# Six homes for expert weights, router products inside the residual products, and a final stage on three engines

## The chip, the cores and the metric

The kernel runs on one core of a Trainium2 chip. A core has TensorE (PE), VectorE (DVE), ScalarE (ACT), GpSimd (POOL) and SyncE (SP). They run at the same time and wait for each other on semaphores. Here nearly all loads are issued by SP, and some stores and all row-wise gathers and scatters by GpSimd. The metric is the device time of one execution in microseconds (us), lower is better.

## The reference

One layer of a hybrid streaming encoder on 640 tokens (512 of a prompt, 8 streams of 16), width 1024, float32. A mixer (state space branch and sparse attention, both gated) is followed by `x = x + merged @ w_o`. Then comes a mixture of experts and a last norm, and the change lies in these:

```python
def moe_sublayer(x, norm_g, w_router_group, b_router_group, w_router_expert, b_router_expert, w1, w3, w2):
    h = rmsnorm(x, norm_g)
    glog = h @ w_router_group + b_router_group          # 4 groups
    p_group = softmax(glog)[argmax(glog)]
    elog = h @ w_router_expert + b_router_expert        # 8 experts a group
    top_v, top_i = top_k(elog of the chosen group, 2)
    top_w = softmax(top_v) * p_group
    for e in range(32):                                 # 1024 -> 256 -> 1024
        he = silu(h @ w1[e]) * (h @ w3[e])
        y = y + combine[:, e:e+1] * (he @ w2[e])
    return x + y
y_prompt, y_sample = rmsnorm(x, norm_final_g)           # prompt rows, stream rows
```

## The kernel before

Tokens stand in `NT` = 5 tiles of 128 rows (`P`), four of the prompt and one of the streams. Each engine's program is written out by hand, in one block, and engines meet at semaphores; the order of a program is the order of the code. The change touches the last four stages.

**Residual products.** For tile `tt`, TensorE makes `merged @ w_o` in two halves of 512 columns (`x1_half`, L1601; each 8 contraction blocks, `k`), into one PSUM bank each. VectorE adds the residual (`residual`, L2709). TensorE transposes the new rows (`rows_turned`, helper line L1438), VectorE copies them with a gain (`turned_rows`, L2717). ScalarE squares the row (L2083), VectorE and ScalarE make its root (`scale`: variance, root, Newton steps), ScalarE writes the scaled row to `xn` (L2087) and GpSimd stores it to `x_rows` in HBM (L1128).

**Routing.** TensorE's router product (`router`, L1618, 36 columns) reads the transposed rows. VectorE's `select_dve` (L2377 to L2405, some 20 small instructions, one behind the other) picks two experts per token. TensorE counts each token's rank within its expert (`ranked`, L1625 and L1627), VectorE's `place_dve` makes one-hot rows of it, and TensorE's `placed` (L1636) sums them into the table of slots. VectorE reads that table as row numbers (L2425 to L2431). PSUM banks are given out by `plan_banks` in the order of these calls.

**Experts.** Each expert has 64 slots. GpSimd gathers its rows (L1135, `rows_in`, a ring of `RS` = 4), TensorE transposes them (`turned`), makes the products with `w1` and `w3` (`up`, L1701), the transposed hidden rows, and the product with `w2` (`down`, L1717). ScalarE copies the result to `ysl` (L2102, also `RS` buffers), GpSimd scatters it to `y_rows` in HBM (L1149). The weights are loaded by SP, two 1 MB blocks for `w1` and `w3` (`load13`, L936) and one for `w2` (`load2`, L940), into `XS` = 5 homes. These are parts of SBUF that earlier stages have done with, so each becomes free at its own time. From expert 5 on, a load waits until the expert five before it has been used:

```python
for e in range(XS, NE):
    sp.wait_ge(S["up_full"], e - XS + 1)
    load13(e)
    sp.wait_ge(S["dn_full"], e - XS + 1)
    load2(e)
```

**Final stage.** When the last scatter has landed, SP loads each token's two result rows (`ypart`, L733, ten loads of 512 KB). VectorE adds them, weighted by `wk`, to the residual row (`sums`, L783 and L785), ScalarE squares (L748), a root and Newton steps follow per group of tiles (`FINAL`: 0 and 1, 2 and 3, 4), and VectorE multiplies by the root and the gain `fin_row` (L775). SP stores (L738). A second copy of this stage, for tokens beyond their expert's 64 slots, stands in a branch that isn't taken here.

## Time and profile before

| what | value |
|---|---|
| median of 3 runs | 1481.96 us (1479.64 to 1481.99) |
| the profiled execution | 1481.5 us |
| its span, first to last instruction | 1480.0 us |
| mean granted TensorE clock | 0.957 of full speed |
| busy share of the span | TensorE 91%, VectorE 53%, ScalarE 33%, GpSimd 16% |
| moved | 247.47 MB, 167 GB/s on average |

All rows and times below are of the profiled execution, in us from the start of its span. Shares are averages over very different stages, so the stages are read one by one, in windows. In a timeline, what stands in brackets is how long the engine had been idle before the row and which instruction released it; "issue" means that the profile shows no releaser.

### The profile page before, as it was taken

To read this page: it belongs to the slowest core of one execution; us is meant where nothing else is said; L and a number is where in the kernel's file an instruction comes from. 1 tells how busy PE (TensorE), PEld (TensorE's weight loads), DVE (VectorE), ACT (ScalarE), POOL (GpSimd) and SP (SyncE) were. 2 spreads that over 40 slices of the span, in tenths; PEclk is the share of its full clock that TensorE was granted. 3 is DMA by queue.
4 is the path that set the end of the run, shared out by engine and by line. 5 is a ranking of instruction groups with operands and counts; after the bars stand their busy time and mean duration, and the time that the engine had idled before them with its cause. 6 is when DMAs were issued, how large, how long until landed. Compare 5 with 4: busy or idle time off the path is not lost.

```text
span 1480.0 us, 19513 instructions
## 1 busy us (share of the span) xinstructions
PE 1350.8 (91%) x7218; PEld 912.2 (62%) x7218; DVE 789.6 (53%) x1707; ACT 493.7 (33%) x1155; POOL 234.5 (16%) x334
## 2 busy tenths in 40 slices
PE   7999999999999999998988999999999889778880
PEld 5555666666767767775667777777755545445540
DVE  4258988898899898997645511111114522111105
ACT  2153144655575565437756320000001201111112
POOL 2000000321221231224700000000000033222210
PEclk9999999999999999998999999999999889989995
DMA  8412425335435434435056443133042499999965
GB/s 266 127 36 52 144 86 144 126 107 142 140 94 156 128 120 129 124 123 129 2 116 155 173 122 111 24 113 115 0 182 120 163 350 413 416 415 416 414 275 220
DMA packets 148177, 247.47 MB, mean 167 GB/s; under 512 B 39540, under 2 KB 106852, under 8 KB 139156
## 3 DMA queue, kind: packets, MB, share of 16 engines
q1 hardware_dynamic: 137012, 215.10, 43.6%
q0 software_dynamic: 11072, 31.12, 6.0%
q8 instruction: 59, 0.97, 0.3%
q14 instruction: 34, 0.28, 0.1%
HBM read 216.50 MB, written 36.88 MB: 171 GB/s over the span
## 4 chain that ended last, share of the span: by engine, by line
PE 61%; DVE 9%; ACT 4%; issue 3%; DMA 1%; SPq 0%; DVEq 0%; POOLq 0%; ACTq 0%
PE psum L669 17%; PE psum L1434 14%; PE psum L1701 9%; PE psum L1601 5%; PE psum L1438 5%; PE psum L1717 4%; PE psum L1385 1%; PE psum L1325 1%; ACT arena L1937 1%; PE psum L1337 1%; DVE arena L2613 1%; PE psum L1370 1%; DVE ssq L2612 1%; DVE arena L2756 1%; DVE arena L2220 1%
## 5 line engine op out<-in xcount | busy, mean ns | idle before, releaser
L669 PE MATMUL psum<-hT,wring 128*128 128x320 f32 x1024 | 289.1, 435 | 2.6 <-ACT wring L645 2.2
L669 PEld LDWEIGHTS psum<-hT,wring 128*128 128x128 f32 x1024 | 192.6, 190 | 85.7 <-ACT wring L645 5.3
L669 PE MATMUL psum<-wring 128*128 128x320 f32 x768 | 217.4, 433 | 0.0
L669 PEld LDWEIGHTS psum<-wring 128*128 128x128 f32 x768 | 145.8, 190 | 61.3 <-ACT wring L645 0.8
L1438 PE MATMUL psum<-ident,arena 128*128 128x128 f32 (+3 forms) x950 | 138.4, 285 | 28.9 <-ACT arena L1937 11.9
L1438 PEld LDWEIGHTS psum<-ident,arena 128*128 128x128 f32 (+3 forms) x950 | 105.9, 143 | 81.5 <-issue 54.8
L1434 PE MATMUL psum<-arena,wring 128*128 128x320 f32 x512 | 138.1, 431 | 0.0
L1434 PEld LDWEIGHTS psum<-arena,wring 128*128 128x128 f32 x512 | 96.6, 189 | 41.2
L1701 PE MATMUL psum<-wring,arena 128*64 128x256 f32 x608 | 86.0, 446 | 24.2 <-issue 20.6
L645 ACT ACTIVATE wring<-psum 128x320 f32<-128x320 f32 (+2 forms) x140 | 50.0, 379 | 168.6 <-PE psum L669 168.0
L1937 ACT ACTIVATE arena<-psum 128x512 f32<-128x512 f32 (+8 forms) x155 | 73.1, 520 | 69.9 <-PE psum L1438 43.5
L2763 DVE TENSOR_TENSOR arena<-psum,arena 128x128 f32<-128x128 f32 x32 | 9.3, 292 | 160.6 <-ACT arena L2094 157.3
L1701 PEld LDWEIGHTS psum<-wring,arena 128*64 128x64 f32 x608 | 55.6, 161 | 50.1 <-issue 29.4
L2083 ACT ACTIVATE arena<-arena 128x1024 f32<-128x1024 f32 x5 | 5.3, 1057 | 232.3 <-DVE arena L2709 232.3
L2128 DVE SCALAR_TENSOR_TENSOR arena<-arena,pc 128x664 f32<-128x664 f32 x72 | 74.2, 1031 | 2.6
L2690 DVE TENSOR_TENSOR arena<-psum,arena 128x320 f32<-128x320 f32 x16 | 7.9, 492 | 119.0 <-PE psum L1434 119.0
L1128 POOL DMA_DIRECT2D x_rows<-arena x5 | 2.7, 546 | 431.5 <-ACT arena L2087 431.5
L1434 PE MATMUL psum<-oT,wring 128*128 128x320 f32 x256 | 69.2, 432 | 0.0
L2094 ACT ACTIVATE arena<-psum 128x128 f32<-128x128 f32 x32 | 8.9, 277 | 177.6 <-PE psum L1701 174.4
L2612 DVE MAX8 ssq<-arena 128x8 f32<-128x1040 f32 (+3 forms) x80 | 66.5, 831 | 1.8
L2613 DVE MATCH_REPLACE8 arena<-ssq,arena 128x1040 f32<-128x1040 f32 (+3 forms) x80 | 65.2, 816 | 0.0
L1149 POOL DMA_INDIRECT y_rows<-arena,slot_row x32 | 32.4, 1011 | 183.9 <-ACT arena L2102 152.7
(344 smaller groups left out, 1993.1 us busy)
## 6 DMA issues: line engine op xcount, KB each, us to landing
wring<-in_w SPq DMA_DIRECT2D x38, 1024.0 KB
arena<-in_w SPq DMA_DIRECT2D x32, 1024.0 KB
wring<-in_w_in SPq DMA_DIRECT2D x25, 1024.0 KB, 5.5
oT<-in_w SPq DMA_DIRECT2D x14, 1024.0 KB
hT<-in_w SPq DMA_DIRECT2D x12, 1024.0 KB
arena<-a_rows SPq DMA_DIRECT2D x20, 512.0 KB, 4.0
arena<-in_state_ssm SPq DMA_DIRECT2D x16, 512.0 KB, 7.3
out<-arena POOLq DMA_DIRECT2D x16, 512.0 KB, 3.9
```

The source lines that it names most:

```text
L645: ins = nc.scalar.activation(v, bank(key + (n,))[:, a:b], ACT.Copy)
L669: ins = nc.tensor.matmul(o[:, 0:TH], wt[:, k, :], rows[:, k, :], start=n in (1, 5, 2) and k == 0, stop=k == 3, skip_group_check=True)
L1149: pool.indirect_dma_start(y_rows[:, :], bass.IndirectOffsetOnAxis(ap=slot_row[:, e:e + 1], axis=0), ysl[:, e % RS, :], None, bounds_check= ...
L1434: ins = mm(out, chunk[:, k, m0:m0 + m], rhs(k), start=first and k == 0, stop=last and k == ks - 1)
L1438: return nc.tensor.transpose(out, in_, ident[0:rows, 0:rows])
L1601: ins = mm(o, mrg[:, k, t * P:(t + 1) * P], ws[n][:, k, :], start=k == 0, stop=k == KD - 1)
L1701: ins = mm(pbank(2 + e % 2)[h * SLOTS:(h + 1) * SLOTS, 0:FF].rearrange("p (c f) -> p c f", c=2), hgT[:, e % 2, k, :], w13[e % XS][:, :, k, ...
L1717: ins = mm(pbank(4 + e % 2)[m * SLOTS:(m + 1) * SLOTS, :], heT[:, e % 2, k, :], w2s[e % XS][:, k, HD2 * m:HD2 * (m + 1)], start=k == 0, st ...
L1937: release(fn(out, in_, ACT.Copy), key)
L2128: ins = stt(out=a, in0=r[:, w:w + 664], scalar=cw_col[:, w, ct:ct + 1], in1=a, op0=ALU.mult, op1=ALU.add)
L2612: link(nc.vector.max(top8, scores))
L2613: link(nc.vector.match_replace(scores, top8, scores, TAKEN))
```

## The change

There are six homes instead of five, each `w2` home in two halves with a load each (the sixth one's lie in what is left of `hTf` and `oTf`). The homes of the `w2` blocks 1 and 2 move out of `mrg`, the input of the residual products, into space of their own, so SP issues the loads of experts 0 to 2 and the `w2` block of 5 before these products. `rows_in` and `ysl` become rings of three; `hgT` and `fin_row` move. In the residual products, transposes, rank and router products of the tile before are issued between two of a half's 8 contraction blocks, each into a bank of its own. (The profile counts two instructions for each float32 product.) In the final stage ScalarE and GpSimd take tile 2's sum, and the scaling of tiles 0 to 2 (ScalarE by the root, GpSimd by the gain); GpSimd stores these three tiles, and VectorE keeps the rest. The result rows of tile 2 are loaded second.

```diff
-XS = 5
-RS = 4
+XS = 6
+RS = 3
...
         w2_first, x1 = a5.take(2 * D), a5.take(NT, D)
-        h2T, xn = a5.take(2, KD, P), a5.take(3, D)
-        rows_in, hgT, ysl = a5.take(RS, HD2), a5.take(2, KD, SLOTS), a5.take(RS, HD2)
+        h2T, xn, w2_more = a5.take(2, KD, P), a5.take(3, D), a5.take(4 * D)
+        hgT = xn[:, 2, :].rearrange("p (u k q) -> p u k q", u=2, k=KD)
...
+        rows_in, ysl_last = a5.take(RS, HD2), a5.take(HD2)
+        ysl = [arena[:, 4 * D:4 * D + HD2], arena[:, 4 * D + HD2:5 * D], ysl_last]
 
         wringf = wring.rearrange("p s k n -> p s (k n)")
         w13 = [v.rearrange("p (c k f) -> p c k f", c=2, k=KD) for v in
-               (wringf[:, 1], oTf[:, 0:2 * KD * FF], wringf[:, 2], wringf[:, 0], hTf[:, 0:2 * KD * FF])]
-        w2s = [v.rearrange("p (k n) -> p k n", k=2) for v in
-               (w2_first, arena[:, 0:2 * D], arena[:, 2 * D:4 * D], xn.rearrange("p t d -> p (t d)")[:, 0:2 * D],
+               (wringf[:, 1], oTf[:, 0:2 * KD * FF], wringf[:, 2], wringf[:, 0], hTf[:, 0:2 * KD * FF], arena[:, 0:2 * KD * FF])]
+        w2s = [[v[:, 0:D], v[:, D:2 * D]] for v in
+               (w2_first, w2_more[:, 0:2 * D], w2_more[:, 2 * D:4 * D], xn.rearrange("p t d -> p (t d)")[:, 0:2 * D],
                 h2T.rearrange("p u k q -> p (u k q)"))]
+        w2s.append([hTf[:, 2 * KD * FF:KD * T], oTf[:, 2 * KD * FF:KD * T]])
         squares_out = oTf.rearrange("p (t d) -> p t d", t=NT)
-        nothing = ssq[:, 5, 7:8]
-        fin_row = arena[:, 4 * D:5 * D]
+        nothing, root_table = ssq[:, 5, 7:8], ssq[:, 5, 6:7]
+        fin_row = kvtm[:].rearrange("p t w -> p (t w)")[:, 0:D]
...
-            for tt in range(NT):
+            for tt in (0, POOL_TILE, 1, 3, 4):
                 for c in range(2):
...
+        POOL_TILE = 2
+
+        def final_pool(pool, r, link):
+
+            done = NT + 5 * r
+            pool.wait_ge(S["hx_scaled"], done + 1)
+            link(nc.gpsimd.tensor_tensor(sums[:, POOL_TILE, :], ypart[:, POOL_TILE, 0, :], x1[:, POOL_TILE, :], ALU.add))
+            pool.wait_ge(S["hx_scaled"], done + 2)
+            nc.gpsimd.tensor_tensor(sums[:, POOL_TILE, :], ypart[:, POOL_TILE, 1, :], sums[:, POOL_TILE, :], ALU.add) \
+                .then_inc(S["pool_parts"], 1)
+            pool.wait_ge(S["fin_loaded"], 16)
+            for tt in range(3):
+                pool.wait_ge(S["hx_scaled"], done + 2 + tt + 1)
+                link(nc.gpsimd.tensor_tensor(sums[:, tt, :], sums[:, tt, :], fin_row, ALU.mult))
+                pool.dma_start(y_prompt[0, tt * P:(tt + 1) * P, :], sums[:, tt, :]).then_inc(xn_stored[tt], 16)
...
+            act.wait_ge(tile_loaded[POOL_TILE], 32 + 32 * (r + 1))
+            for c in range(2):
+                part = ypart[:, POOL_TILE, c, :]
+                nc.scalar.activation(part, part, ACT.Copy, scale=wk[:, c, POOL_TILE:POOL_TILE + 1])                     .then_inc(S["hx_scaled"], 1)
+            squares(1, S["parts_added"], parts + 2)
+            roots(0)
+            squares(POOL_TILE, S["pool_parts"], r + 1)
+            scaled(0, (0,))
+            squares(3, S["parts_added"], parts + 3)
+            scaled(0, (1,))
+            roots(1)
+            squares(4, S["parts_added"], parts + 4)
+            roots(2)
+            scaled(1, (POOL_TILE,))
...
+            for tt in (0, 1):
+                first(tt)
+                second(tt)
+            first(3)
+            variances(0)
+            second(3)
+            scaled(0)
+            first(4)
+            variances(1)
+            second(4)
+            scaled(1)
+            finished(3)
+            variances(2)
+            scaled(2)
+            finished(4)
...
-                sp.dma_start(w2s[e % XS], w2[e].rearrange("(k p) n -> p k n", p=P)).then_inc(w2_loaded[e % XS], 16)
+                for k in range(2):
+                    sp.dma_start(w2s[e % XS][k], w2[e, k * P:(k + 1) * P, :]).then_inc(w2_loaded[e % XS], 16)
...
-            load13(0)
-            load2(0)
-            load13(1)
-            load13(2)
-            wait_read(sp, ("x1", NT - 1, 1))
-            load2(1)
+            for e in range(3):
+                load13(e)
+                load2(e)
+            load2(5)
+            wait_full(sp, ("x1", NT - 1, 0))
             load13(3)
-            load2(2)
+            wait_full(sp, ("x1", NT - 1, 1))
             load13(4)
             wait_full(sp, ("rt", NT - 1))
+            load2(4)
             rows_stored(sp)
             sp.wait_ge(gathered_rows[0], 16)
             load2(3)
-            load2(4)
+            load13(5)
...
+            pool.wait_ge(S["t_full"], 1)
+            gather(RS)
             for e in range(NE):
-                if e + RS < NE:
-                    pool.wait_ge(S["t_full"], e + 1)
-                    gather(e + RS)
+                if e + RS + 1 < NE:
+                    pool.wait_ge(S["t_full"], e + 2)
+                    gather(e + RS + 1)
                 pool.wait_ge(S["dn_read"], e + 1)
...
-            def x1_half(t, n):
+            def x1_half(t, n, between):
                 o = claim(pe, ("x1", t, n))
                 for k in range(KD):
+                    if k in between:
+                        between[k]()
...
-                if tt < NT:
-                    x1_half(tt, 0)
-                if 0 < tt < NT:
-                    rows_turned(tt - 1, 1)
-                if 1 < tt < NT:
-                    ranked(tt - 2)
-                if tt < NT:
-                    x1_half(tt, 1)
-                    rows_turned(tt, 0)
-                if tt == NT - 1:
-                    rows_turned(tt, 1)
+            for tt in range(NT):
+                first, second = {}, {5: lambda: rows_turned(tt, 0)}
                 if tt > 0:
-                    router(tt - 1)
-                if 1 < tt < NT:
+                    first[3] = lambda: rows_turned(tt - 1, 1)
+                    second[2] = lambda: router(tt - 1)
+                if tt > 1:
+                    first[6] = lambda: ranked(tt - 2)
+                x1_half(tt, 0, first)
+                x1_half(tt, 1, second)
+                if tt > 1:
                     placed(tt - 2)
             ranked(NT - 2)
+            rows_turned(NT - 1, 1)
+            router(NT - 1)
+            placed(NT - 2)
             ranked(NT - 1)
-            placed(NT - 2)
             placed(NT - 1)
             o = claim(pe, ("tot",))
             pe.wait_ge(S["hot_ready"], 2 * NT)
...
             for tt in range(NT + 1):
-                if tt < NT:
-                    residual(tt, 0)
-                if 0 < tt < NT:
+                if tt > 0:
                     turned_rows(tt - 1, 1)
                     scale(tt - 1)
                 if tt < NT:
-                    residual(tt, 1)
-                    turned_rows(tt, 0)
-                if tt == NT - 1:
-                    turned_rows(tt, 1)
-                    scale(tt)
+                    residual(tt, 0)
+                if 1 < tt < NT:
+                    place_dve(dve, tt - 2, link)
                 if tt > 0:
                     select_dve(dve, tt - 1, link)
-            place_dve(dve, NT - 2, link)
+                if tt < NT:
+                    turned_rows(tt, 0)
+                    residual(tt, 1)
```

The rows of TensorE's program for the last tile, before: L1601 are residual products of a half, L1438 transposes, L1618 the router product of a tile (tile 3, then tile 4), L1625 and L1627 ranks, L1636 slot sums.

```order
L1601 MATMUL psum<-hT,arena 128x512 x8
L1438 MATMUL psum<-ident,arena 128x128 x8
L1618 MATMUL psum<-arena 128x36 x8
L1636 MATMUL psum<-arena 128x32 x2
L1618 MATMUL psum<-arena 128x36 x8
L1625 MATMUL psum<-arena,cum_p 128x32
L1627 MATMUL psum<-arena,ones 128x32
L1625 MATMUL psum<-arena,cum_p 128x32
L1627 MATMUL psum<-arena,ones 128x32
L1636 MATMUL psum<-arena 128x32 x4
L1680 MATMUL psum<-arena,ones 128x32
```

The same place of TensorE's program in the changed kernel (L1685 residual products, L1520 transposes, L1702 router, L1709 and L1711 ranks, L1720 slot sums):

```order
L1685 MATMUL psum<-hT,arena 128x512 x2
L1702 MATMUL psum<-arena 128x36 x8
L1685 MATMUL psum<-hT,arena 128x512 x3
L1520 MATMUL psum<-ident,arena 128x128 x4
L1685 MATMUL psum<-hT,arena 128x512 x3
L1720 MATMUL psum<-arena 128x32 x2
L1709 MATMUL psum<-arena,cum_p 128x32
L1711 MATMUL psum<-arena,ones 128x32
L1520 MATMUL psum<-ident,arena 128x128 x4
L1702 MATMUL psum<-arena 128x36 x8
L1720 MATMUL psum<-arena 128x32 x2
L1709 MATMUL psum<-arena,cum_p 128x32
```

The first router product (tile 3) has moved from behind the last half to behind its second contraction block, and four transposes to behind its fifth; one router product is left behind the products.

SP's program from the first expert load on, before (L936 is `load13`, L940 `load2`, 128x2x1024 is a whole `w2` block):

```order
L936 DMA wring<-in_w 128x2048 x2
L940 DMA arena<-in_w 128x2x1024
L936 DMA oT<-in_w 128x2048 x2
L936 DMA wring<-in_w 128x2048 x2
L940 DMA arena<-in_w 128x2x1024
L936 DMA wring<-in_w 128x2048 x2
L940 DMA arena<-in_w 128x2x1024
L936 DMA hT<-in_w 128x2048 x2
L940 DMA arena<-in_w 128x2x1024 x2
L963 DMA arena<-in_norm_final_g 128x1024
```

And in the changed kernel (L1013 `load13`, L1018 halves of `load2`):

```order
L1013 DMA wring<-in_w 128x2048 x2
L1018 DMA arena<-in_w 128x1024 x2
L1013 DMA oT<-in_w 128x2048 x2
L1018 DMA arena<-in_w 128x1024 x2
L1013 DMA wring<-in_w 128x2048 x2
L1018 DMA arena<-in_w 128x1024 x2
L1018 DMA hT<-in_w 128x1024
L1018 DMA oT<-in_w 128x1024
L1013 DMA wring<-in_w 128x2048 x2
L1013 DMA hT<-in_w 128x2048 x2
L1018 DMA arena<-in_w 128x1024 x4
L1013 DMA arena<-in_w 128x2048 x2
```

Before, the first four rows, seven blocks, stand ahead of the first wait; now the first eight rows, ten blocks, do. The `load13` of experts 3 and 4 now follow one behind each half of the last product, and the sixth home's `load13` stands in the row `arena<-in_w 128x2048 x2`.

GpSimd's program behind its last scatter (first row) held nothing but the end; it now has, in the changed kernel (`wring` is `ypart`, `hT` is `sums`, `kvtm` is `fin_row`):

```order
L1229 DMA y_rows<-arena,slot_row 2560x512 x5
L753 TENSOR_TENSOR hT<-wring,arena 128x1024
L755 TENSOR_TENSOR hT<-wring,hT 128x1024
L760 TENSOR_TENSOR hT<-hT,kvtm 128x1024
L761 DMA out<-hT 128x1024
L760 TENSOR_TENSOR hT<-hT,kvtm 128x1024
L761 DMA out<-hT 128x1024
L760 TENSOR_TENSOR hT<-hT,kvtm 128x1024
L761 DMA out<-hT 128x1024
```

Its two sums of tile 2 come first, and three times a multiplication with the gain and a store have moved here from VectorE and SP.

## Rows read from the trace of the kernel before

**Rows 1.** Page, part 2: GB/s moved in 40 slices of 37 us

```profile
GB/s 266 127 36 52 144 86 144 126 107 142 140 94 156 128 120 129 124 123 129 2 116 155 173 122 111 24 113 115 0 182 120 163 350 413 416 415 416 414 275 220
```

**Rows 2.** Windows: stretch, length, each engine's busy us, granted clock, DMA share, GB/s

```profile
1120.00:1160.00 40.00, 40.00 (x140) 21.33 (x139) 19.81 (x82) 7.01 (x8) 1.07 (x2) 1.00 0.07 27
1172.00:1188.00 16.00, 8.56 (x40) 8.02 (x39) 10.71 (x52) 3.46 (x2) 1.97 (x3) 0.51 1.02 403
1192.00:1214.00 22.00, 21.29 (x154) 12.08 (x154) 5.08 (x11) 2.64 (x8) 4.08 (x4) 0.90 0.93 347
1220.00:1420.00 200.00, 167.76 (x1131) 101.35 (x1129) 34.62 (x98) 28.94 (x79) 49.97 (x50) 0.91 1.02 415
```

**Rows 3.** Timeline, SP's queue: start, duration, line, transfer, count

```profile
1097.38 0.99 SPq L936 DMA_DIRECT2D wring<-in_w  x2
1169.76 0.38 SPq L940 DMA_DIRECT2D arena<-in_w  x1
...
1190.57 0.89 SPq L940 DMA_DIRECT2D arena<-in_w  x2
...
1198.10 0.82 SPq L936 DMA_DIRECT2D wring<-in_w  x2
```

**Rows 4.** Timeline, products to first expert; in brackets idle time and its releaser

```profile
1161.82 7.11 PE L1601 MATMUL psum<-hT,arena 128*128 128x512 f32 x16
...
1168.77 0.60 PE L1438 MATMUL psum<-ident,arena 128*128 128x128 f32 x4
...
1169.04 0.69 DVE L2709 TENSOR_TENSOR arena<-psum,arena 128x512 f32<-128x512 f32 x1 [4.63 <-PE psum L1601]
...
1170.29 1.87 PE L1618 MATMUL psum<-arena 128*128 128x36 f32 x16
...
1172.47 0.25 DVE L2377 SCALAR_TENSOR_TENSOR arena<-psum,ssq,brow 128x36 f32<-128x36 f32 x1
...
1176.95 0.26 DVE L2377 SCALAR_TENSOR_TENSOR arena<-psum,ssq,brow 128x36 f32<-128x36 f32 x1
...
1184.47 0.19 DVE L2425 TENSOR_SCALAR arena<-psum 128x32 f32<-128x32 f32 x1 [1.15 <-PE psum L1636]
...
1186.25 1.12 POOL L1135 DMA_INDIRECT arena<-x_rows,src_row  x1 [10.78 <-DVE slot_row L2431]
...
1190.63 1.94 PE L1438 MATMUL psum<-ident,arena 128*128 128x128 f32 x8 [5.77 <-DMA arena<-x_rows,src_row]
```

**Rows 5.** Timeline, last two experts and last scatter

```profile
1427.55 5.36 PE L1701 MATMUL psum<-wring,arena 128*64 128x256 f32 x32 [2.00 <-issue]
...
1435.29 3.67 PE L1701 MATMUL psum<-oT,arena 128*64 128x256 f32 x32 [0.40 <-issue]
...
1444.66 0.98 POOL L1149 DMA_INDIRECT y_rows<-arena,slot_row  x1 [1.17 <-ACT arena L2102]
```

**Rows 6.** Timeline, final stage

```profile
1447.10 4.99 SPq L733 DMA_DIRECT2D wring<-y_rows  x10
1452.42 1.28 DVE L783 SCALAR_TENSOR_TENSOR hT<-wring,wk,arena 128x1024 f32<-128x1024 f32 x1 [12.82 <-DMA wring<-y_rows]
...
1457.58 1.06 ACT L748 ACTIVATE oT<-hT 128x1024 f32<-128x1024 f32 x1 [1.37 <-DVE hT L785]
...
1474.61 1.28 DVE L775 SCALAR_TENSOR_TENSOR hT<-hT,ssq,arena 128x1024 f32<-128x1024 f32 x1
```

**Rows 7.** GpSimd's groups by form: count, then busy us and mean ns

```profile
L1123 POOL TENSOR_TENSOR arena<-arena 128x512 f32<-128x512 f32 x16 | 16.1, 1039 | 4.5 <-DVE arena L2344 4.5
...
L1123 POOL TENSOR_TENSOR arena<-arena 128x128 f32<-128x128 f32 x16 | 6.0, 398 | 40.3 <-DVE arena L2344 40.3
```

**Rows 8.** Timelines of VectorE and of GpSimd around 312 us

```profile
308.80 2.80 DVE L2128 SCALAR_TENSOR_TENSOR arena<-arena,pc 128x664 f32<-128x664 f32 x3
...
312.11 5.85 DVE L2128 SCALAR_TENSOR_TENSOR arena<-arena,pc 128x664 f32<-128x664 f32 x3
...
311.65 5.60 POOL L1044 TENSOR_TENSOR arena<-arena 128x640 f32<-128x640 f32 x3 [1.88 <-ACT arena L1881]
```

137 lines of the change are left out of this document (80 added, 57 removed).

## Prediction

> **What bounds the kernel now.** I read the page's slices first. For five slices, from about 1221 us on, the chip moves 413 to 416 GB/s, and nowhere else does it come near that for so long [rows 1]. This is the expert stage: 32 experts, each with three weight blocks of 256 x 1024 x 4 bytes = 1.049 MB. The windows say the same with the engines beside it: from 1220 to 1420 the DMA share is 1.02 and the rate 415 GB/s, while TensorE is busy 168 of 200 us [rows 2]. So a block costs 1.049 MB / 415 GB/s = 2.53 us, and the stage ends when its bytes have been moved. The timeline of its end agrees: the last two up products begin after idle times that no engine released, 2.00 and 0.40 us, that is, when weights land [rows 5]. The same windows show the stretch that is wasted: from 1120 to 1160, in the residual products, the rate is 27 GB/s [rows 2]. SP's queue shows why. Its last early load goes out at 1097.38, and the next waits until 1169.76 for a free home [rows 3]. By then 7 blocks are in (three up pairs, one down block).
>
> The second thing is the stretch from the last product to the first expert. TensorE's last product half begins at 1161.82; select for tile 3 runs at 1172.47 and for tile 4 at 1176.95; the slot numbers are read at 1184.47; the first gather is issued at 1186.25 and its rows are transposed at 1190.63 [rows 4]. SP's next loads go out with that landing, at 1190.57 [rows 3].
>
> Third, the final stage. From the last scatter at 1444.66 [rows 5] all is serial. VectorE begins at 1452.42 and ends at 1474.61 + 1.28 = 1475.89, 23.5 us later [rows 6]; the span ends 4.1 us after that.
>
> **The loads.** After the change 10 blocks go out early instead of 7 (experts 0 to 2 complete, and the down block of 5). The three more cost 7.6 us of transfer at about 1117 to 1125, where 27 GB/s says that nobody needs the queue [rows 2]; without that cover they would cost the same 7.6 us. Home 3 is released a half product earlier, homes 4 and the down block 4 during the routing. So before the first gather is back, 15 blocks are in against 13: 2 x 2.53 = **5.1 us** less to move afterwards. The third early block is not worth more than that, because the down blocks of 1 and 2, which filled the routing stretch (1.02 busy from 1172 to 1188 [rows 2]), now leave it idle from about 1180.
>
> After the gather, before: 2 down blocks and the gain row, then nothing until up product 0 is done at 1198.10 [rows 3]. The share from 1192 to 1214 is 0.93 against 1.02 in full flow, (1.02 - 0.93) x 22 = 2.0 us of gaps [rows 2]. With home 5, three blocks and the row last 3 x 2.53 + 1.3 = 8.9 us, and up product 0 ends some 7.5 us after them, so the queue doesn't run dry. I keep 0.4 us for latency: **1.6 us** gained.
>
> **The router.** In the order before, the router product of tile 3 (1.87 us [rows 4]) stands behind all products, so that two selects of 1176.95 - 1172.47 = 4.5 us follow each other. After, it stands inside the last product half. That half starts at about 1161.9 as before, gets 1.87 us of router and some 0.4 us of transposes, and ends near 1171.2 instead of 1168.8. Select 3 runs beside it, from 1161.9 + 2 x 0.88 + 1.87 = 1165.5 to 1170.0. Then, for tile 4: residual, transposes and their copy, 0.7 us each [rows 4], to 1173.5; the placing of tile 3, now between, and the Newton steps, four and five small VectorE instructions, about 1.0 us each, to 1175.8; select 4 ends at 1180.2 instead of 1181.4. One placing instead of two follows, 0.9 us less. The slot numbers come at 1182.4 instead of 1184.5, **2.1 us** earlier.
>
> The gather took 1190.6 - 1186.25 = 4.3 us, issued while the weight queue was still full [rows 2, 4]. The last scatter, in an idle queue, was through when SP issued the next loads: 1447.10 - 1444.66 = 2.4 us [rows 5, 6]. After the change the queue is idle by 1180, so I take 2.4: **1.9 us**. The bound on the other side is 0.
>
> Everything in the expert stage then moves by 5.1 + 1.6 + 2.1 + 1.9 = **10.7 us**. Rings of three instead of four for gathered rows and results cost nothing: gather e+4 still goes out after the same scatter, and a result row waits for the scatter of three experts ago, at least 3 x 6.0 us old, while the last one landed in 2.4 us. The down loads as two halves keep rows of 4 KB and the same bytes.
>
> **The final stage.** VectorE loses two 1024-wide steps of tile 2 and three closing ones, 5 x 1.28 = 6.4 us. ScalarE gets two scalings before and three after, each like its Square of 1.06 us [rows 6]; GpSimd two additions and three multiplications. Their form isn't in the trace. GpSimd's multiply takes 398 ns at 128 columns and 1039 at 512 [rows 7], so an estimate for 1024 is 1039 + 4 x 641 / 3 = 1894 ns.
>
> If the three engines ran freely, from the landing of tile 0 as zero: VectorE sums tile 0 to 2.5, must wait until 5.1 for tile 1 (now third in the queue, 2.53 us a tile), is done with it at 7.6, with tile 3 and the first Newton steps at 11.3; ScalarE's Square of tile 3 comes at 13.6, tile 4 is summed at 15.0, scaled steps 15.9, tile 3 closed 17.2; then variance and root, ScalarE's scaling of tile 2 to 18.7, GpSimd's multiply to **20.7**. Against 23.5 that is 2.8 us less.
>
> But they don't run freely. Three VectorE steps of 664 columns take 2.80 us alone and 5.85 beside three GpSimd operations, which take 5.60 instead of the 3 x 1.25 that rows 7 give for 640 columns [rows 7, 8]. A pair costs 1.95 where the sum is 0.93 + 1.25 = 2.18: they take turns, with 0.25 us saved per pair. All of VectorE's sums here read two tiles in SBUF, and all of GpSimd's do. Played through with turns, VectorE waits 1.5 us before tile 1, 1.6 in the middle of it, 0.5 before the last sum and 1.4 in the second Newton steps (behind the multiply of tile 1), and GpSimd's last multiply waits 1.1 for VectorE's last row: 20.7 + 6.1 = 26.8, less 0.3, by which the same playing-through overstates the stage before. 26.5 - 23.5 = **3.0 us more**, with the store behind it taken as long as before. I take this end, since rows 8 are two engines on the very kinds of operands. The bounds are -2.8 (free) and +4.5 (no overlap per pair at all).
>
> The Trainium skill, page "SBUF — State Buffer", section "Who interferes with whom", says that a VectorE instruction with two SBUF inputs contends with a GpSimd instruction that reads SBUF, and one of them blocks. By it the final stage gets longer; a count of engine work alone would make it shorter. The trace agrees, with 5.85 against 2.80 us.
>
> **The sum.** 1480.0 - 10.7 + 3.0 = 1472.3 for the span; the profiled execution took 1481.5, 1.5 more than its span: 1473.8. The median of the runs, 1481.96, is 0.5 above that execution: **1474.3 us**. What a measurement here can tell from no change is about 0.2%, 3 us.
>
> **Rivals.** (1) The engines overlap freely in the final stage: -2.8 instead of +3.0, 1468.5. For it: GpSimd's 1.9 us are an extrapolation. Against it: rows 8. 15%. (2) The stage is tied to the first gather alone and its transfers gain only half: no faster gather and no closed gaps, 3.5 us less, 1478. For it: gathers compete with whatever is queued; the new order leaves the queue idle at 1180. 16%. (3) The change doesn't deliver bytes: TensorE, busy 168 of 200 us, becomes the limit of the stage. It needs 3.67 us for an up product [rows 5] and some 2.4 for the rest of an expert, 6.1 us at full clock, against at least 3 x 2.53 = 7.6 us of transfers, so it would have to run long at half clock. Then only the router's 2.1 us remain against the 3.0, 1482.9. 7%. (4) Slower: router and transposes now stand in the middle of accumulations, and TensorE can't go on past them. The router of tile t-1 needs VectorE's transposed copy, which stands behind the second residual and, before that, behind a 4.5 us select. If select is still running there, each of four tiles stretches: it decides from 7.5 / 4 = 1.9 us a tile on; the whole select each time is 4 x 4.5 = 18 us, 1492. Against it: select ends at 1170.0 in my count, the router of the next tile would come after more than 8 us. 5%. My forecast, 57%, has a range of its own of 1471 to 1478.
>
> Range 1467.5 to 1480 with (1) and (2) and the edge of (3). Faster by over 0.2%: the forecast, (1) and three quarters of (2), 0.84; within 0.2%: 0.10; slower 0.06.
>
> **What would show it.** SP's early loads end at about 1125 and a load goes out near 1162, before the last product half. One select, not two, stands behind the products; the first gather lands near 1186.6. The share from 1192 to 1420 is 1.02 without gaps. The last up product starts near 1424.6 instead of 1435.3. In the final stage, GpSimd's 1024-wide operations take well over 1.9 us, VectorE's over 1.28, and the last store is GpSimd's. I am wrong if product halves take longer than 7.1 us plus what is inserted, or if the last up product comes less than 7 us earlier.

## The result and the profile after

The changed kernel takes 1486.95 us (median of 8 runs, 1483.62 to 1489.28) against 1481.12 us before (8 runs beside it): ratio 1.0045, 95% interval 1.003 to 1.006. It is slower, by 5.8 us in the medians (4 to 9 by the interval), where 1474.3 was predicted. Its profiled execution took 1486.17 us with a span of 1484.5; up to 1096 us the two traces run within 0.2 us of each other.

The page's slices and the windows of the changed kernel, for [rows 1, 2] (stretch, length, busy time of each engine, granted clock, DMA share, GB/s):

```profile
GB/s 267 125 41 48 142 88 142 132 100 143 139 105 144 141 106 136 116 123 129 2 133 140 171 152 97 6 114 113 0 222 178 175 386 414 415 416 415 412 211 131
```

```profile
1120.00:1160.00 40.00, 40.00 (x147) 21.78 (x145) 18.66 (x72) 9.18 (x12) 1.07 (x2) 1.00 0.24 96
1172.00:1188.00 16.00, 5.35 (x34) 4.89 (x32) 7.95 (x38) 4.51 (x5) 2.96 (x4) 0.61 0.64 241
1192.00:1214.00 22.00, 21.30 (x163) 11.79 (x159) 4.78 (x14) 2.92 (x9) 4.89 (x5) 0.99 1.01 412
1220.00:1420.00 200.00, 169.93 (x1162) 102.78 (x1162) 34.79 (x98) 29.71 (x81) 49.87 (x50) 0.92 1.01 410
```

The bytes have moved as foreseen: 96 instead of 27 GB/s beside the residual products, and 412 instead of 347 GB/s from 1192 to 1214, with no gaps. From 1172 to 1188 the share fell from 1.02 to 0.64. The 410 GB/s of the last window, against 415 before, is not a lower rate: the stage now ends inside the window. From 1220 to 1400 the changed kernel moves 414 GB/s and the kernel before 415; from 1415 to 1420 it is 258 against 411.

The timeline of the changed kernel around the routing and the first gather, for [rows 3, 4] (start, duration, engine, line, operation; in brackets idle time and what ended it):

```profile
1161.91 0.81 SPq L1013 DMA_DIRECT2D wring<-in_w  x2
...
1165.35 0.26 DVE L2458 SCALAR_TENSOR_TENSOR arena<-psum,ssq,brow 128x36 f32<-128x36 f32 x1 [1.73 <-PE psum L1702]
...
1171.01 0.80 SPq L1013 DMA_DIRECT2D hT<-in_w  x2
...
1177.41 0.53 POOL L1206 DMA_DIRECT2D x_rows<-arena  x1 [15.26 <-ACT arena L2168]
...
1182.02 0.19 DVE L2506 TENSOR_SCALAR arena<-psum 128x32 f32<-128x32 f32 x1 [1.15 <-PE psum L1720]
...
1184.96 1.11 POOL L1213 DMA_INDIRECT arena<-x_rows,src_row  x1 [7.02 <-DMA x_rows<-arena]
...
1188.47 0.80 SPq L1018 DMA_DIRECT2D arena<-in_w  x2
1188.53 2.30 PE L1520 MATMUL psum<-ident,arena 128*128 128x128 f32 x8 [6.12 <-DMA arena<-x_rows,src_row]
```

A load goes out at 1161.91, select for tile 3 begins at 1165.35 inside the last product, the home of the last product half is free at 1171.01 (predicted: 1171.2), and the slot numbers are read at 1182.02 instead of 1184.47. But the first gather is issued only at 1184.96, 2.94 us after the slot numbers where it was 1.78 before: it waits for the store of the last rows (issued 1177.41), which costs 1.2 us. SP, which waits for that gather, goes on at 1188.47, 3.51 us after the issue, and TensorE transposes the rows at 1188.53. Before it was 1190.57 - 1186.25 = 4.32 [rows 3, 4]. So in an idle queue the gather is 0.8 us faster, not 1.9. How full the queue was just then, before and after:

```profile
1184.00:1190.00 6.00, 0.86 (x5) 0.73 (x4) 0.89 (x5) 0.00 (x0) 3.14 (x3) 0.50 0.89 361
```

```profile
1184.00:1190.00 6.00, 1.37 (x6) 1.00 (x7) 0.34 (x1) 0.00 (x0) 3.15 (x3) 0.50 0.35 74
```

The end of the expert stage, for [rows 5]:

```profile
1426.69 3.67 PE L1782 MATMUL psum<-oT,arena 128*64 128x256 f32 x32 [2.10 <-issue]
```

```profile
1436.06 0.98 POOL L1229 DMA_INDIRECT y_rows<-arena,slot_row  x1 [1.17 <-ACT arena L2183]
```

The last up product begins at 1426.69 instead of 1435.29, the last scatter at 1436.06 instead of 1444.66: 8.6 us earlier both.

Then it is lost. VectorE and GpSimd in the final stage, for [rows 6]:

```profile
1443.71 1.28 DVE L840 SCALAR_TENSOR_TENSOR hT<-wring,wk,arena 128x1024 f32<-128x1024 f32 x1 [12.71 <-DMA wring<-y_rows]
...
1448.77 3.37 DVE L840 SCALAR_TENSOR_TENSOR hT<-wring,wk,arena 128x1024 f32<-128x1024 f32 x1 [2.45 <-DMA wring<-y_rows]
1452.17 3.25 DVE L845 SCALAR_TENSOR_TENSOR hT<-wring,wk,hT 128x1024 f32<-128x1024 f32 x1
...
1461.26 1.37 DVE L852 TENSOR_SCALAR ssq<-ssq 128x2 f32<-128x2 f32 x1 [1.01 <-ACT oT L770]
...
1463.92 2.12 DVE L822 TENSOR_TENSOR ssq<-ssq 128x2 f32<-128x2 f32 x1
```

```profile
1448.71 2.34 POOL L753 TENSOR_TENSOR hT<-wring,arena 128x1024 f32<-128x1024 f32 x1 [11.68 <-ACT wring L793]
1451.14 3.20 POOL L755 TENSOR_TENSOR hT<-wring,hT 128x1024 f32<-128x1024 f32 x1
1460.26 2.35 POOL L760 TENSOR_TENSOR hT<-hT,kvtm 128x1024 f32<-128x1024 f32 x1 [5.92 <-ACT hT L783]
...
1469.37 3.36 POOL L760 TENSOR_TENSOR hT<-hT,kvtm 128x1024 f32<-128x1024 f32 x1 [2.46 <-ACT hT L783]
1473.03 0.57 POOL L761 DMA_DIRECT2D out<-hT  x1 [0.30 <-POOL hT L760]
```

From the first sum, 1443.71, to the end of GpSimd's last multiply, 1469.37 + 3.36 = 1472.73, it is 29.0 us, against 23.5 before. VectorE's steps beside GpSimd's show 3.37 and 3.25 instead of 1.28, and two steps on 128 x 2 numbers, 0.16 to 0.17 us before, show 1.37 and 2.12. GpSimd's five operations show 2.34 to 3.36.

After the last store lies something of which the prediction knew nothing. The block's closing drains of SP and of GpSimd, changed kernel first, then GpSimd's in the kernel before (duration in ns three times, then start):

```profile
L2864 SPq DRAIN  x1: 13/13/13, 1476.2 to 1476.2; - x1
L2864 POOLq DRAIN  x1: 7093/7093/7093, 1476.2 to 1476.2; - x1
```

```profile
L2785 POOLq DRAIN  x1: 6848/6848/6848, 1447.3 to 1447.3; - x1
```

When its program ends, GpSimd drains for 7.09 us. Before, this took 6.85 us from 1447.3, behind a final stage that lasted until 1478.5; nobody waited for it. Now GpSimd is the last to finish (1476.2), and the whole program waits: SP's waits show it.

```profile
SPq L2864 <- PEq L2864: 7.3, 1, 7.3
```

The row names TensorE's sequencer as the one that released SP. TensorE's own drain was over at 1434.7; the only one that ends just before SP goes on, at 1483.3, is GpSimd's.

The difference of the spans adds up: -8.6 (experts) - 0.1 + 5.5 (29.0 - 23.5) + 0.6 (the last store, 3.2 us from the end of the multiply to its landing instead of 2.65) + 7.1 (8.5 us instead of 1.4 from landing to the end) = +4.5 = 1484.5 - 1480.0.

### The profile page after: what moved, and what is told of

It reads as the page before. It is cut to its first block, busy times and chain, and to the rows that moved or that the text cites. A ratio compares the mean times of both kernels' runs of the same rounds, so it can differ in the third digit from the quotient of the medians.

```text
span 1484.5 us, 19556 instructions
## 1 busy us (share of the span) xinstructions
PE 1344.2 (91%) x7218; PEld 906.5 (61%) x7218; DVE 791.7 (53%) x1702; ACT 498.9 (34%) x1161; POOL 249.1 (17%) x342
## 4 chain that ended last, share of the span: by engine, by line
PE 59%; DVE 8%; ACT 4%; issue 4%; DMA 2%; POOL 0%; SPq 0%; ACTq 0%; DVEq 0%; POOLq 0%
PE psum L672 17%; PE psum L1516 14%; PE psum L1782 9%; PE psum L1520 4%; PE psum L1685 4%; PE psum L1798 4%; PE psum L1467 1%; PE psum L1407 1%; ACT arena L2018 1%; PE psum L1419 1%; DVE arena L2694 1%; PE psum L1452 1%; DVE ssq L2693 1%; DVE arena L2301 1%; ACT arena L2122 1%
## 5 line engine op out<-in xcount | busy, mean ns | idle before, releaser
L1520 PE MATMUL psum<-ident,arena 128*128 128x128 f32 (+3 forms) x950 | 138.7, 285 | 28.7 <-ACT arena L2018 11.6
L1520 PEld LDWEIGHTS psum<-ident,arena 128*128 128x128 f32 (+3 forms) x950 | 105.8, 143 | 81.6 <-issue 54.0
L1782 PE MATMUL psum<-wring,arena 128*64 128x256 f32 x512 | 67.6, 423 | 15.8 <-issue 12.3
L1782 PEld LDWEIGHTS psum<-wring,arena 128*64 128x64 f32 x512 | 44.0, 152 | 35.6 <-issue 17.9
```

The source lines that it names most:

```text
L1520: return nc.tensor.transpose(out, in_, ident[0:rows, 0:rows])
L1782: ins = mm(pbank(2 + e % 2)[h * SLOTS:(h + 1) * SLOTS, 0:FF].rearrange("p (c f) -> p c f", c=2), hgT[:, e % 2, k, :], w13[e % XS][:, :, k, ...
```

## Experiments

Thirteen kernels. The first four ran together, with the kernel before at 1481.56 us beside them.

**e1: GpSimd's end moved late in the kernel before.**

```diff
             for i in range(RS):
                 pool.wait_ge(scattered[i], 16 * NE // RS)
+            pool.wait_ge(S["fin_ready"], NT)
```

> The kernel before with one line more: GpSimd, at the end of its program, waits for VectorE's last closed row. Nothing else changes, and nobody waits for GpSimd there. Theory A (the end of the block costs GpSimd a drain of about 7 us once its program is over, and in the kernel before that lay behind the final stage): the drain begins at 1475.9 instead of 1447.3, ends at 1482.8, and the span is about 1484.0, +4.0 us, ratio 1.0027. Theory B (the 8.5 us after the last landing in the changed kernel belong to its stores, which go through GpSimd's own software queue): no change, 0 us, since no store is moved here.

Measured: 1487.14 us, ratio 1.0039 (1.0026 to 1.0053). Its drain, by the source line:

```profile
L2786 POOLq DRAIN  x1: 6848/6848/6848, 1474.5 to 1474.5; - x1
```

In the profiled execution the last row was closed at 1474.26 and the span ended at 1482.7, 8.4 us later; before it was 4.1 [rows 6]. So +4.3 there, and the interval (3.9 to 7.9 us) holds the 4.0. A single wait that delays no work costs what of the drain the last store no longer hides: theory A.

**e2: the final stage of before, everything else as changed.** The functions of the final stage are those of the kernel before (with the gain row and the homes where the changed kernel has them); GpSimd's part is gone.

> The changed kernel with the final stage of before (VectorE and ScalarE only, all stores from SP); six homes and the router inside the products stay. Theory A (expert stage 8.6 us earlier, all of the loss lies in the final stage and the drain): 8.6 us less than the kernel before, ratio 0.994, execution about 1472.9. Theory B (the six homes also slow the final stage, through the gain row in another buffer or the rows of results elsewhere): less than 6 us gained.

Measured: 1472.83 us, ratio 0.9944 (0.993 to 0.9957). 8.7 us less than before: the 8.6 us of the expert stage are whole, and theory A holds.

**e3: the other half, the new final stage alone on the kernel before.**

> The kernel before with only the final stage of the changed kernel (tile 2 and the closing of rows 0 to 2 on GpSimd, its stores from its own queue). Theory A (the parts add up): +5.5 for the engines, +0.6 for the store, +7.1 for the drain, together +13.2 us, ratio 1.009. Theory B (what the prediction counted, turns of VectorE and GpSimd only): +3.0 us, ratio 1.002.

Measured: 1495.30 us, ratio 1.0092 (1.0078 to 1.0106). The first sum and the last multiply:

```profile
1452.99 1.28 DVE L837 SCALAR_TENSOR_TENSOR hT<-wring,wk,arena 128x1024 f32<-128x1024 f32 x1 [12.68 <-DMA wring<-y_rows]
```

```profile
1478.67 3.36 POOL L757 TENSOR_TENSOR hT<-hT,arena 128x1024 f32<-128x1024 f32 x1 [2.46 <-ACT hT L780]
```

Again 1482.03 - 1452.99 = 29.0 us, and 13.7 us lost in all: theory A. The two halves of the change add up within the intervals: +13.7 and -8.7 give +5.0, the changed kernel shows +5.8.

**e4: SP issues the stores of GpSimd's rows.**

```diff
-                link(nc.gpsimd.tensor_tensor(sums[:, tt, :], sums[:, tt, :], fin_row, ALU.mult))
-                pool.dma_start(y_prompt[...], sums[:, tt, :]).then_inc(xn_stored[tt], 16)
+                nc.gpsimd.tensor_tensor(sums[:, tt, :], sums[:, tt, :], fin_row, ALU.mult).then_inc(S["pool_parts"], 1)
```

> The changed kernel, with the three stores of GpSimd's rows issued by SP, so that GpSimd's program ends with its last multiply at about 1472.7. Theory A (a drain of fixed length follows the end of the program, whatever was queued): it runs from 1472.8 to 1479.9 beside the last store, and the span ends near 1481.1, 3.4 us less than the changed kernel, so about 1 us over the kernel before. Theory B (the drain is long because software-queue stores are young): it gets short, and the span ends 1.5 us after the last landing, near 1477, 7 us less than the changed kernel. Also: if issuing stores costs GpSimd time between its multiplies, those come closer together by up to 0.5 us each.

Measured: 1482.36 us, ratio 1.0002 (0.9993 to 1.0011), 4.6 us under the changed kernel.

```profile
L2860 POOLq DRAIN  x1: 10280/10280/10280, 1469.4 to 1469.4; - x1
```

This drain starts beside the last multiply, so 3.4 of its 10.3 us are that; it then works on for 6.9 us. Theory A's time, and theory B falls: here GpSimd's last transfer was 33 us old. (That the length is fixed, as theory A has it, e8 refutes.) The multiplies came no earlier without the stores between them: GpSimd's first two now follow each other directly, but VectorE's second sum of tile 4 is held beside them, 3.44 instead of 1.27 us, and the last multiply begins at 1469.48, as before the edit (1469.37).

**e5: six homes and moved loads, the router's steps in their old order, old final stage.** The loops of TensorE, VectorE and the bank plan over the residual products are those of before.

> Six homes and moved transfers alone: the final stage of before, and the router's steps back in the order of before (no insertion into accumulations). The sum of the prediction gives homes and loads 5.1 + 1.6 and the router 2.1, of which 8.6 were seen together. Theory A (the parts add as in the trace: slot numbers 2.4 us late again): 8.6 - 2.4 = 6.2 us under the kernel before, ratio 0.9958. Theory B (stage bound by bytes alone; the order of the router hardly matters, since the queue was idle for 5 us before the first gather): the full 8.6, 0.9942.

Measured: 1474.79 us, ratio 0.9958 (0.9945 to 0.9971), beside 1480.89 before. The new order of the router is worth 0.9958 - 0.9944 = 0.0014, 2.1 us, with an uncertainty of about the same size (0.0018); theory A's 0.9958 fits. Theory B's 0.9942 lies just outside this interval, but a difference from e2 isn't clear of noise.

**e6: the down block in one transfer again**, on e2.

```diff
-                for k in range(2):
-                    sp.dma_start(w2s[e % XS][k], w2[e, k * P:(k + 1) * P, :]).then_inc(w2_loaded[e % XS], 16)
+                if e % XS == XS - 1:
+                    ...
+                else:
+                    sp.dma_start(w2_home[e % XS].rearrange("p (k n) -> p k n", k=2),
+                                 w2[e].rearrange("(k p) n -> p k n", p=P)).then_inc(w2_loaded[e % XS], 16)
```

> Six homes, new router order, final stage of before (as the run with the old final stage, 1472.8), but the down block loads as one transfer again wherever its home is in one piece (5 homes of 6). Theory A (the halves cost rate: 410 instead of 415 GB/s from 1220 to 1420): 415 GB/s is back and the last up product comes 2 us earlier, 1470.8. Theory B (the rate has another cause): 1472.8 and still 410 GB/s.

Measured: 1472.36 us, ratio 0.9938 (0.9921 to 0.9954). Its window up to 1400:

```profile
1220.00:1400.00 180.00, 152.99 (x1047) 91.40 (x1043) 31.53 (x92) 26.87 (x73) 46.74 (x46) 0.92 1.02 414
```

Nothing gained that can be told: the halves cost nothing measurable, as predicted. Theory A's premise was a misreading. In the window from 1220 to 1420 this kernel shows 408 GB/s, again because its end already lies in the run-out (214 GB/s from 1415 to 1420); up to 1400 it moves 414, as e2 and the changed kernel do with halves.

**e7: the store of the last rows ahead of a weight block**, on e2.

```diff
-            load2(4)
             rows_stored(sp)
+            load2(4)
             sp.wait_ge(gathered_rows[0], 16)
```

> As the run with the old final stage (1472.8), but the down block of expert 4 goes out after the store of the last router rows has landed, not before it. Theory A (the store landed at 1184.0 since it stood behind that block; it held the first gather back): the store lands near 1181, the first gather is issued near 1183.2 instead of 1185.0 and its rows are back near 1186.7, but it competes with the block: up to 1.8 us gained, 1471.0 to 1472.8. Theory B (the gather then waits for the block instead): no change.

Measured: 1473.07 us, ratio 0.9948 (0.9935 to 0.996): nothing gained that can be told. The first gather of e2, then of e7:

```profile
1184.52 1.12 POOL L1139 DMA_INDIRECT arena<-x_rows,src_row  x1 [5.86 <-DVE slot_row L2437]
...
1188.03 2.35 PE L1445 MATMUL psum<-ident,arena 128*128 128x128 f32 x8 [4.91 <-DMA arena<-x_rows,src_row]
```

```profile
1180.81 7.08 SPq L944 DMA_DIRECT2D arena<-in_w  x4
...
1183.72 1.12 POOL L1139 DMA_INDIRECT arena<-x_rows,src_row  x1 [5.85 <-DVE slot_row L2437]
...
1187.21 2.19 PE L1445 MATMUL psum<-ident,arena 128*128 128x128 f32 x8 [4.88 <-DMA arena<-x_rows,src_row]
```

The store has landed when SP goes on at 1180.81, as theory A says. But the edit had nothing to win: in e2's profiled execution the gather already went out behind the slot numbers and not behind the store, as it does here (1.8 us after their first reading in both). Of the ten profiles with the new router order four show a wait for the store: the changed kernel and e9 1.1 to 1.2 us, e11 and e12 0.2 to 0.3.

The gather itself, from its issue until SP or TensorE goes on, took 4.2 to 4.5 us in the four profiles with five homes (before, e1, e3, e8), where the weight queue is full, and 3.4 to 3.5 us in ten with six homes, where it runs idle (e11, below, is the eleventh). So the queue is worth some 0.7 to 1.1 us of its price, not 1.9.

**e8: two drains in the kernel before.**

```diff
             for i in range(RS):
                 pool.wait_ge(scattered[i], 16 * NE // RS)
+            pool.drain()
+            pool.wait_ge(S["fin_ready"], NT)
```

> The kernel before, with GpSimd waiting for VectorE's last closed row at the end of its program (as in the first experiment, +5.6 us), and with one explicit drain instruction ahead of that wait, after the last scatter, where GpSimd is idle. Theory A (a drain costs about 6.9 us whatever came before it): the end is as late as in the first experiment, span 4 to 5 us over the kernel before. Theory B (a drain works off what GpSimd issued since the last one, transfers above all): the early one takes the 6.9 us in the shade, the second takes well under 1 us, and the time is that of the kernel before.

Measured: 1480.95 us, ratio 1.0001 (0.9992 to 1.0011): the 5.6 us of e1 are gone. The explicit drain and the block's own:

```profile
L1155 POOLq DRAIN  x1: 6848/6848/6848, 1446.4 to 1446.4; - x1
```

```profile
L2787 POOLq DRAIN  x1: 40/40/40, 1475.7 to 1475.7; - x1
```

Theory B. A drain works off what came before it: 6.85 us for the first, 0.04 for the second.

**e9: the early drain in e4. e10: the early drain alone in the changed kernel** (`pool.drain()` ahead of `final_pool(pool, 0, link)` in both).

> The changed kernel with GpSimd's three stores issued by SP, and one explicit drain on GpSimd behind its last scatter, where it is idle for some 10 us before tile 2's first addition. Theory (a drain works off the transfers that GpSimd issued since the last one; two drains in the kernel before left 0.04 us for the second): the block's own drain gets short, and the span ends 1.5 us after the last store's landing, 4.2 us earlier than with SP's stores alone: about 1478, ratio 0.9975. Against it: the drain takes 6.9 us for GpSimd's arithmetic too, then 1482 as before, or later by what the early drain holds back.

> The changed kernel with one line more: the explicit drain on GpSimd behind its last scatter. GpSimd keeps its three stores. It tells what the last drain costs after three plain transfers. Theory A (its length goes with how many transfers were issued since the last one, over a hundred before): well under 1 us, the span 6.5 us less than the changed kernel's, 1480. Theory B (any transfer since the last drain costs the whole 7 us): no change, 1486.5.

Measured: e9 1477.89 us, ratio 0.9972 (0.9961 to 0.9983); e10 1478.61 us, ratio 0.9981 (0.997 to 0.9992), beside 1481.86. The block's own drains, e9 and e10:

```profile
L2861 POOLq DRAIN  x1: 3472/3472/3472, 1468.0 to 1468.0; - x1
```

```profile
L2865 POOLq DRAIN  x1: 287/287/287, 1473.7 to 1473.7; - x1
```

e9's 3.47 us lie beside the last multiply (3.36 us), so arithmetic leaves next to nothing to drain. Three plain transfers leave 0.29 - 0.04 = 0.25 us, 0.08 us each; 7.09 - 6.85 = 0.24 in the changed kernel is the same. e10 gained more than the 6.8 us of the drain (0.0064 of 1481.9 is 9.5 us, 7 to 12 by the intervals); its last scatter came at 1433.7 instead of 1436.1 in the profiled execution, which the drain behind it can't have caused (its first gather didn't wait for the store and went out at 1183.3 instead of 1185.0). The last scatter of kernels with the same expert stage lies between 1430.7 (e13) and 1436.1, so differences of 2 us between single profiles are not read here. One line turns the changed kernel from 0.45% slower to 0.19% faster.

**e11: the queue's idle stretch filled, and one wait of VectorE removed**, on e2.

```diff
             rows_stored(sp)
+            load2(3)
             sp.wait_ge(gathered_rows[0], 16)
-            load2(3)
```

and in the final stage the variances of rows 0 and 1 behind the first sum of tile 2, not behind the second sum of tile 1.

> As the run with the old final stage (1472.8), with two edits in separate stages. First, the down block of expert 3 goes out before the first gather is back (from 1184, where the queue is idle until 1187) instead of behind it: theory A, one block (2.8 us) less to move afterwards, minus 0 to 2 us by which the first gather is held up, so the last up product comes 1 to 2.8 us earlier; theory B, the gather is held up as long as the block takes, nothing gained. Second, in the final stage VectorE reads the squares of rows 0 and 1 one sum later, and so doesn't wait 1.2 us for ScalarE: the stage from the first sum to the last closed row takes 22.4 instead of 23.6 us. Together 1469 to 1471.6.

Measured: 1471.40 us, ratio 0.993 (0.9914 to 0.9945), the fastest kernel of all, though its interval overlaps with e2's. Windows of e2, then of e11:

```profile
1200.00:1204.00 4.00, 4.00 (x31) 1.94 (x29) 0.98 (x2) 1.04 (x3) 0.00 (x0) 1.00 0.98 403
```

```profile
1200.00:1204.00 4.00, 4.00 (x29) 2.00 (x27) 0.98 (x2) 1.04 (x3) 0.00 (x1) 1.00 0.89 299
```

And e11's gather, issued at 1183.95:

```profile
1188.65 0.80 SPq L945 DMA_DIRECT2D arena<-in_w  x2
```

Theory B's outcome, in two ways. The gather was held up, but by less than the block takes: 4.7 us beside the block, against 3.45 in e2. And the block moved into the gap leaves a gap behind the gather: SP's next load waits for up product 0 at 1195.4 in both, and the share falls to 0.89. From the slot numbers to the last up product it is 243.1 us, against 243.3 in e2. The final stage took 23.4 instead of 23.7 us; tile 1 landed 1.07 us late for VectorE, which took most of the 1.2.

**e12: VectorE reads one operand from PSUM**, on e9.

```diff
+            for tt in (0, 1, 3, 4):
+                if tt == 4:
+                    act.wait_ge(S["dn_read"], NE)
+                nc.scalar.activation(rows_at(tt), x1[:, tt, :], ACT.Copy).then_inc(S["r_exp"], 1)
...
-                link(stt(out=sums[:, tt, :], in0=ypart[:, tt, 0, :], scalar=wk[:, 0, tt:tt + 1],
-                         in1=x1[:, tt, :], op0=ALU.mult, op1=ALU.add))
+                link(stt(out=rows_at(tt), in0=ypart[:, tt, 0, :], scalar=wk[:, 0, tt:tt + 1],
+                         in1=rows_at(tt), op0=ALU.mult, op1=ALU.add))
```

> As the run with SP's stores and the early drain (1477.9; final stage from the first sum to the last multiply 29 us), but VectorE reads only one tile in SBUF in each of its 1024-wide steps: in the 7.6 us between the last scatter and the first sum ScalarE, idle there, copies the residual rows of tiles 0, 1, 3 and 4 into PSUM (and later the gain row), the first sum is written in place there, and the second reads it from there. The arithmetic and GpSimd's five operations stay. Theory A (VectorE's steps with two tiles in SBUF and GpSimd's take turns): without the second SBUF tile VectorE's steps stay at 1.3 us beside GpSimd, and the stage takes the 21.1 us of free overlap with GpSimd's measured 2.35 us an operation, 7.9 us less: 1470. Theory B (GpSimd's operations and the order of waits set the length, not the turns; or they collide in SBUF whatever VectorE's second operand is): VectorE's steps still show 3.1 to 3.4 us beside GpSimd's, and the stage stays at 28 to 29 us, 1477 to 1478.

Measured: 1472.34 us, ratio 0.9938 (0.9918 to 0.9958), 5.6 us under e9.

```profile
1439.91 1.29 DVE L849 SCALAR_TENSOR_TENSOR psum<-wring,wk,psum 128x1024 f32<-128x1024 f32 x1 [12.42 <-DMA wring<-y_rows]
...
1446.17 1.29 DVE L849 SCALAR_TENSOR_TENSOR psum<-wring,wk,psum 128x1024 f32<-128x1024 f32 x1 [3.65 <-DMA wring<-y_rows]
1447.50 1.28 DVE L854 SCALAR_TENSOR_TENSOR hT<-wring,wk,psum 128x1024 f32<-128x1024 f32 x1
...
1454.61 1.37 DVE L861 TENSOR_SCALAR ssq<-ssq 128x2 f32<-128x2 f32 x1 [1.00 <-ACT oT L771]
...
1457.27 1.02 DVE L829 TENSOR_TENSOR ssq<-ssq 128x2 f32<-128x2 f32 x1
```

```profile
1447.30 2.35 POOL L759 TENSOR_TENSOR hT<-wring,hT 128x1024 f32<-128x1024 f32 x1
...
1461.62 2.34 POOL L764 TENSOR_TENSOR hT<-hT,kvtm 128x1024 f32<-128x1024 f32 x1 [3.34 <-ACT hT L784]
```

VectorE's wide steps stay at 1.28 and 1.29 us, and GpSimd's second sum takes 2.35 beside them where it took 3.20. Theory A for these. Two small steps with all operands in SBUF are still held, 1.37 and 1.02 us instead of 0.17. The stage takes 1463.96 - 1439.91 = 24.05 us: 5 less than 29.0, not the 7.9 of theory A. Of the 3 us that are left, an estimate from the rows: tile 1 is begun 6.3 us after the first sum where the free sum had 5.1 (it lands third, and VectorE stood 3.65 us before it), and the two small steps lost 1.2 and 0.9 us.

**e13: tile 1 loaded second**, on e12. What was open then, on record before the run: whether the 24.05 us come from the order of loads or from GpSimd's own chain.

```diff
-            for tt in (0, POOL_TILE, 1, 3, 4):
+            for tt in (0, 1, POOL_TILE, 3, 4):
...
-            first(3)
             variances(0)
+            first(3)
             second(3)
```

> As the run with rows in PSUM (1472.3; final stage 24.05 us from the first sum to the last closed row), with tile 1's results loaded second instead of third, and ScalarE's and VectorE's steps in the order in which the tiles now land (squares of 1 before the scaling of tile 2; variances of 0 and 1 before tile 3). Theory A (what is left over the freely overlapping 21 us is waiting for loads: VectorE stood idle 3.65 us before tile 1): the stage takes 19.6 to 21 us, 3 to 4.4 us less, 1468 to 1469.3. Theory B (GpSimd's own chain sets the end, and tile 2 now lands 1.2 us or more later, which moves its last multiply back by that): 24 us or more, no gain.

Measured: 1473.51 us, ratio 0.9944 (0.993 to 0.9959); no gain.

```profile
1437.90 1.29 DVE L849 SCALAR_TENSOR_TENSOR psum<-wring,wk,psum 128x1024 f32<-128x1024 f32 x1 [12.30 <-DMA wring<-y_rows]
...
1441.48 1.29 DVE L849 SCALAR_TENSOR_TENSOR psum<-wring,wk,psum 128x1024 f32<-128x1024 f32 x1 [0.97 <-DMA wring<-y_rows]
...
1449.32 1.87 DVE L829 TENSOR_TENSOR ssq<-ssq 128x2 f32<-128x2 f32 x1
```

```profile
1446.39 2.35 POOL L757 TENSOR_TENSOR hT<-wring,arena 128x1024 f32<-128x1024 f32 x1 [14.76 <-ACT wring L801]
...
1461.12 2.35 POOL L764 TENSOR_TENSOR hT<-hT,kvtm 128x1024 f32<-128x1024 f32 x1 [3.35 <-ACT hT L784]
```

VectorE's wait before tile 1 fell from 3.65 to 0.97 us, but GpSimd's first sum comes 8.5 us after VectorE's instead of 5.0, and three of VectorE's small steps now fall beside GpSimd's operations: 1.87, 1.37 and 1.01 us. The stage takes 25.6 us. Theory B, with that second cause added.

## Why the prediction was wrong

**Loads, 5.1 + 1.6.** The mechanism held: 15 blocks before the gather, share 1.01 behind it. From SP's first load behind the gather to the last up product it was 1435.29 - 1190.57 = 244.7 us for 83 blocks [rows 3, 5] and is 1426.69 - 1188.47 = 238.2 us for 81: 6.5 us, where 6.7 was forecast. That it fits so well is in part luck. The prediction divided by 415 GB/s, which also carries gathers and scatters; over the stretch a block takes 2.92 us before, without the 2.0 us of gaps, and 2.94 after. Two blocks at that price are 5.9 us, not 5.1, and with the gaps 7.5; why 1.0 of this didn't come is open.

**Router, 2.1.** 2.45 us at the slot numbers, slightly more than forecast. But 1.2 of them were lost in this execution to the store of the last rows, a wait that the prediction didn't have; e2, with the same code there, didn't wait for it. e5 gives about 2 us in the runs' medians, hardly clear of noise.

**First gather, 1.9.** The direction was right and the size wrong. The step took 2.4 us from a scatter in an idle queue and put all of the gather's other 1.9 us down to the full one. In an idle queue it took 3.5 us: 0.8 us less than before. The expert stage fell short by 2.1 us (-8.6 instead of -10.7): 1.1 at the gather, 1.2 at the store, 0.2 at the loads, less 0.35 that the router gave more.

**Rings and half loads, 0.** Right for the halves by e6. The rings weren't tried apart; no wait for them shows inside the stage.

**Final stage, +3.0.** The turns are there, as forecast from [rows 8]. The Trainium skill, page "SBUF — State Buffer", section "Who interferes with whom", says that a VectorE instruction with two SBUF inputs contends with GpSimd's reads and one with at most one SBUF input, outside its 2-port modes, doesn't; the traces agree for VectorE's second sum, with 3.25 us in e9 against 1.28 in e12. The mis-sized term is GpSimd's operation: extrapolated 1.89 us, measured 2.35 where nothing holds it. The trace of before warned of it: the shortest of its 128 x 640 operations took 1312 ns, where the straight line of [rows 7] gives 1253. Row by row, the prediction had waits of 1.5, 1.6, 0.5, 1.4 and 1.1 us, 6.1 in all; the rows show 2.1, 2.0, 1.2, 2.0 and 1.0 us above the free durations, 8.3 in all. The difference of 2.2 us is nearly the whole miss of this term, 29.0 against 26.5.

**Not in the sum: the drain, +7.1.** This is the step that failed, and it decided the sign. The prediction took the 4.1 us behind the last row to follow whoever was last. The early signs of being wrong that the prediction named, longer product halves and a last up product less than 7 us earlier, both looked at the expert stage and stayed silent. The prediction asked of each moved piece what work would hide it, but not of what stood behind GpSimd's last instruction. The Trainium skill, page "VectorE: DVE Perf Modes", section "The DRAIN you can't avoid", has the drains of a kernel's preamble and postamble at a constant 12 ns or so on all five engines; if the block's closing drains are meant, SP's 13 ns agrees and GpSimd's 7093 does not.

**The rivals.** None came true. (1) fell with the turns, (3) and (4) with the expert stage, which did come earlier with its product halves as computed. (2), less gained by transfers and gather, was half right: the gather gave 0.8 of its 1.9 us, the transfers nearly all. The slower side had a mechanism inside the products; the loss lay at the other end. With the drain the prediction's own sum would have been 1474.3 + 7.1 = 1481.4; the remaining 5.5 us are the expert stage with its gather and store (2.1), the longer final stage (2.5), its slower store (0.6) and 0.3 unexplained.

## What to carry to other kernels

Before work is given to an engine that used to finish early, list everything behind its last instruction, the block's closing drain too: an engine that becomes the last one brings its whole tail with it. If GpSimd has issued many transfers, an explicit drain where it is idle takes that tail out (e8 to e10). And a third engine beside VectorE is worth its own rate only if VectorE's operands don't all lie in SBUF: here three engines with turns took 29.0 us, without them on the wide steps 24.05, and two engines 23.5; e2, e6 and e11 (0.6 to 0.7% faster than before), which leave GpSimd out, are at least as fast as e12 with it (0.6%). And before two kernels' windows are compared, see that the stage fills both: 410 against 415 GB/s was only an earlier end.

## What the runs showed of the hardware

- GpSimd's drain took 6.85 us after 141 transfers of its own queue (77 plain, 64 indirect, counted over its DMA rows), 7.09 after 144, 0.29 after three, 0.11 after arithmetic alone (3.47 less the 3.36 of the running multiply), 0.04 after nothing. Arithmetic adds little: e4 has the kernel before's 141 transfers and five operations more, and beyond its last multiply its drain takes the same 6.9 us. At 0.08 us a plain transfer, 77 make 6.3 us; what the indirect ones add wasn't measured apart.
- GpSimd's 128 x 1024 addition or multiplication of two tiles in SBUF takes 2.35 us where nothing holds it, though 128 and 512 columns [rows 7] extrapolate to 1.89.
- A step of VectorE on 128 x 2 numbers beside a GpSimd operation on 1024 columns showed up to 2.12 us instead of 0.16: the small steps of a chain of rows suffer as much as the wide ones.
- A gather of 128 rows of 2 KB by GpSimd took 3.4 to 3.5 us until SP could go on when the weight queue was idle (ten profiles), 4.2 to 4.5 when it was full (four), and 4.7 with a 1 MB block issued just ahead of it (e11).
